# Hybrid decoder step on one core: the output projection's first tile is multiplied, and its second turned, inside the sample stage

## What is computed

```python
h   = rms_norm(x, norm1_g)
proj = h @ w_in                       # attention q, k, v; mLSTM q, k, v, gates
att = dilated attention (8 heads x 64), windows combined by softmax of their log-sums
hb  = mLSTM (4 heads x 128), chunkwise
x   = x + concat(att, hb) @ w_out     # the output projection
x   = x + square(relu(rms_norm(x, norm2_g) @ w_up)) @ w_down
y   = rms_norm(x, norm_f_g)
```

## Time and profile before

| | us |
|---|---|
| median of 3 runs | 2995.48 |
| lowest and highest of them | 2992.3 and 2998.82 |
| the profiled execution | 2989.5 |
| its span, first to last instruction | 2987.7 |

### The profile page before, as it was taken

How to read it: one execution, slowest core, us unless ns; L and a number is a source line. 1 busy time by engine, 2 the same in 40 slices (tenths; PEclk the granted TensorE clock), 3 DMA queues, 4 the chain that set the end, 5 groups by cost and what they waited for, 6 DMA issues and landing times.

```text
span 2987.7 us, 47542 instructions
## 1 busy us (share of the span) xinstructions
PE 2855.3 (96%) x18291; PEld 2478.0 (83%) x18291; DVE 1427.7 (48%) x3363; ACT 926.2 (31%) x1741; POOL 1003.3 (34%) x590
## 2 busy tenths in 40 slices
PE   7999999998999968899999999999999999999997
PEld 5878788887777756678799999989999998899996
DVE  5522555334888845586343333344333333544444
ACT  4301322112767742332132221243212222422222
POOL 1212012211455530210064343444434344545443
PEclk8999999999999988999999999999999999999999
DMA  4322223334464448955352323235222323533332
GB/s 137 113 102 97 97 94 122 106 117 147 133 193 155 160 141 335 370 174 187 134 220 94 126 93 107 94 122 225 94 108 93 126 93 117 207 129 131 138 126 83
DMA packets 124794, 421.41 MB, mean 141 GB/s; under 512 B 18655, under 2 KB 44387, under 8 KB 104918
## 3 DMA queue, kind: packets, MB, share of 16 engines
q1 hardware_dynamic: 103836, 366.53, 34.7%
q10 hardware_dynamic: 19658, 48.68, 4.2%
q0 software_dynamic: 1152, 4.19, 0.5%
HBM read 350.83 MB, written 135.63 MB: 163 GB/s over the span
## 4 chain that ended last, share of the span: by engine, by line
PE 48%; ACT 1%; POOL 1%; DVE 0%; DMA 0%; issue 0%; ACTq 0%
PE mlp_bank L220 16%; PE mlp_bank L221 16%; PE mlp_bank L222 16%; PE mlp_bank L236 0%; PE mlp_bank L235 0%; POOL mlp_wu_lo L2634 0%; DMA mlp_xb<-x 0%; PE mlp_bank L2982 0%; DVE mlp_acc L2854 0%; POOL mlp_xb L2676 0%; ACT mlp_wu_hi L2692 0%; ACT mlp_acc L2767 0%; DVE mlp_hT_lo L2903 0%; DVE mlp_acc L2871 0%; POOL mlp_acc L2681 0%
## 5 line engine op out<-in xcount | busy, mean ns | idle before, releaser
L2854 DVE TENSOR_TENSOR mlp_acc<-mlp_acc,mlp_bank 128x512 f32<-128x512 f32 x542 | 348.2, 684 | 365.7 <-PE mlp_bank L222 357.6
L220 PE MATMUL mlp_bank<-mlp_hT_hi,mlp_wu_hi 128*128 128x384 f32 (+1 forms) x1536 | 496.0, 323 | 3.1 <-PEq L3122 3.1
L222 PE MATMUL mlp_bank<-mlp_hT_hi,mlp_wu_lo 128*128 128x384 f32 (+1 forms) x1536 | 494.6, 322 | 0.0
L221 PE MATMUL mlp_bank<-mlp_hT_lo,mlp_wu_hi 128*128 128x384 f32 (+1 forms) x1536 | 494.4, 322 | 0.0
L2842 DVE TENSOR_TENSOR mlp_xn<-mlp_xn 128x384 f32<-128x384 f32 (+1 forms) x192 | 203.8, 1068 | 509.5 <-ACT mlp_xn L2710 489.3
L220 PE MATMUL mlp_bank<-mlp_wd_hi,mlp_u_hi 128*128 128x512 f32 x1024 | 400.0, 391 | 5.0 <-DVE mlp_acc L2854 5.0
L221 PE MATMUL mlp_bank<-mlp_wd_lo,mlp_u_hi 128*128 128x512 f32 x1024 | 398.9, 390 | 0.0
L222 PE MATMUL mlp_bank<-mlp_wd_hi,mlp_u_lo 128*128 128x512 f32 x1024 | 398.8, 389 | 0.0
L2638 POOL TENSOR_TENSOR mlp_wd_lo<-mlp_wd_raw,mlp_wd_hi 128x2048 fp32r<-128x2048 f32 x48 | 221.8, 4621 | 391.6 <-ACT mlp_wd_hi L2698 391.6
L2647 POOL TENSOR_TENSOR mlp_u_lo<-mlp_xn,mlp_u_hi 128x384 fp32r<-128x384 f32 (+1 forms) x192 | 177.9, 938 | 359.0 <-ACT mlp_u_hi L2719 359.0
L220 PEld LDWEIGHTS mlp_bank<-mlp_hT_hi,mlp_wu_hi 128*128 128x128 f32 x1536 | 288.2, 188 | 5.2 <-issue 3.5
(11 more groups left out here) (370 smaller groups left out, 4693.6 us busy)
## 6 DMA issues: line engine op xcount, KB each, us to landing
mlp_wu_raw<-in_w_up SPq DMA_DIRECT2D x48, 1024.0 KB, 4.9
mlp_wd_raw<-in_w_down SPq DMA_DIRECT2D x48, 1024.0 KB, 4.9
out_win_k_sample<-in_cache_k SPq DMA_DIRECT2D x48, 680.0 KB, 6.3
out_win_v_sample<-in_cache_v SPq DMA_DIRECT2D x48, 680.0 KB, 7.2
p_w_raw<-in_w_tok SPq DMA_DIRECT2D x10, 2048.0 KB
sm_vin<-in_cache_v SPq DMA_DIRECT2D x8, 2048.0 KB, 12.3
proj<-p_stage ACTq DMA_DIRECT2D x53, 256.0 KB, 2.0
parts<-mx_part SPq DMA_DIRECT2D x48, 264.0 KB, 3.9
```

What stands on the lines that cost most here:

```text
L220: nc.tensor.matmul(out, ah, bh, start=(k == 0), stop=False)
L221: nc.tensor.matmul(out, ah, bl, start=False, stop=False)
L222: ins = nc.tensor.matmul(out, al, bh, start=False, stop=(k == n - 1))
L2854: ins = v.tensor_tensor(acc[:, t, 512 * e:512 * e + 512], acc[:, t, 512 * e:512 * e + 512], bank[4 + 2 * (t % 2) + e][:], ALU.add)
```

## The change

- In the sample stage SP issues the weight's last two quarters and the parts of tiles 0 and 1 right behind the values of sequence 6 (in round b = 5), and so ahead of the values of sequence 7. The x rows of tiles 0 to 2 are loaded in the sample stage too, ahead of the 8 stores.
- DVE computes the weights of tile 0 in the second half of sequence 6, its products and sum in the second half of sequence 7. It then also does there the shift of tile 1, lo(0), the rest of the fourth quarter, the combination of tile 1, and lo(1).
- ACT rounds both tiles in the sample stage.
- PE turns tile 0, multiplies its first half, then blocks 0 to 3 of its second half, turns tile 1, and multiplies blocks 4 to 7, all behind the last values product and ahead of the barrier. The output projection's own list starts with products(1, 0).
- The 8 PSUM banks are allocated once for all three stages. The load of tile 2's parts stays in the output projection's block, its condition (tile 0 turned) is met when that block begins.

```diff
@@ class OutHead
+    def load_x(self, sp, t):
+        sp.dma_start(self.xt[t % 3][:], self.K.x[t * P:(t + 1) * P, :]).then_inc(self.x_in[t % 3], 16)
+
+    def turn_first(self, pe, t, bank):
+        pe.wait_ge(self.mixed, t + 1)
+        for k in range(KC):
+            m = (self.ma if k < 4 else self.mb)[t]
+            ins = self.K.nc.tensor.transpose(bank[2 * t + k // 4][:, (k % 4) * P:(k % 4 + 1) * P],
+                                             m[:, (k % 4) * P:(k % 4 + 1) * P], self.K.ident[:])
+        ins.then_inc(self.turned, 1)
+
+    def hi_first(self, act, t, bank):
+        act.wait_ge(self.turned, t + 1)
...
+    def lo_first(self, dve, t, bank):
+        dve.wait_ge(self.hi_ready, t + 1)
...
+    def products_first(self, pe, e, bank, part):
+        cols = slice(512 * e, 512 * e + 512)
+
+        def split(k):
+            if e == 0 and k % 2 == 0:
+                pe.wait_ge(self.w_lo_ready[k // 2], 1)
+
+        if e == 0:
+            pe.wait_ge(self.lo_ready, 1)
+        split_products(self.K.nc, bank[4 + e][:],
+                       [(self.mT_hi[:, 0, k], self.mT_lo[:, 0, k], self.w_hi[:, k, cols], self.w_lo[:, k, cols])
+                        for k in range(KC)], self.prod_mm, split, part=part)
...
@@ mix_sample, block.sync
                 if b:
                     sp.wait_ge(s["summed"], b)
                     load_v(b + 1)
+                if b == 5:
+                    for q in range(2, 4):
+                        O.load_w(sp, q)
+                    for t in range(2):
+                        O.load(sp, t)
...
-            for q in range(2, 4):
-                O.load_w(sp, q)
-            for t in range(2):
-                O.load(sp, t)
+            sp.wait_ge(s["summed"], DEC_B - 1)
+            for t in range(3):
+                O.load_x(sp, t)
             sp.wait_ge(s["o_ready"], DEC_B)
@@ block.scalar
+            O.exp(act, 0)
             probs(DEC_B - 1)
-            O.exp(act, 0)
             O.round(act, 3)
+            O.hi_first(act, 0, bank)
+            O.exp(act, 1)
+            O.hi_first(act, 1, bank)
@@ block.vector
             for b in range(4, DEC_B):
                 first_half(b)
-                second_half(b - 1)
...
+                second_half(b - 1, first_weights if b == DEC_B - 1 else None)
+            second_half(DEC_B - 1, lambda: O.blend(dve, O.chain, 0))
+            O.shift(dve, O.chain, 1)
+            O.lo_first(dve, 0, bank)
+            O.rest(dve, v, 3)
+            O.combine(dve, O.chain, 1)
+            O.lo_first(dve, 1, bank)
@@ block.tensor
             second_half(DEC_B - 1)
+            O.turn_first(pe, 0, bank)
+            O.products_first(pe, 0, bank, range(KC))
+            pe.wait_ge(s["o_ready"], DEC_B)
+            O.products_first(pe, 1, bank, range(4))
+            O.turn_first(pe, 1, bank)
+            O.products_first(pe, 1, bank, range(4, KC))
@@ project_out
-            for t in range(3):
-                load_x(t)
...
-            hi(0)
-            O.exp(act, 1)
...
-            O.rest(dve, v, 3)
-            lo(0)
-            O.shift(dve, chain, 1)
-            O.combine(dve, chain, 1)
...
-            turn(0)
-            for t in range(NP + 1):
+            for t in range(1, NP + 1):
                 products(t, 0)
```

More of the change, by code:

```diff
@@ L1614, in __init__ @@
         self.shifted, self.exps, self.mixed, self.own = (sem("out_" + n) for n in ("shifted", "exps", "mixed", "own"))
+        self.x_in = [sem(f"out_x_in{q}") for q in range(3)]
+        self.turned, self.hi_ready, self.lo_ready, self.prod_mm = (
+            sem("out_" + n) for n in ("turned", "hi", "lo", "prod_mm"))
     def load_w(self, sp, q):
@@ L1655, in combine, with blend @@
         chain.link(v.tensor_tensor(S[:, 2], S[:, 1], S[:, 4, 2:3].broadcast_to([P, 3, H]), ALU.mult))
+    def combine(self, dve, chain, t):
+        self.weights(dve, chain, t)
+        self.blend(dve, chain, t)
+    def blend(self, dve, chain, t):
+        v, p = self.K.nc.vector, t % 2
+        q, S = self.pt[p], self.st[:, p]
+        prod = self.prod if t else self.prod_first
         for a in range(3):
@@ L1830, in mix_sample @@
         sm = rec("sm", NS, 10, MH)
-        bank = [ctx.enter_context(nc.psum_tensor(f"sm_bank{i}", [P, 512], F32)) for i in range(8)]
+        bank = K.bank
         SC, PV, ML = (3, 4), 5, (6, 7)
@@ L2542, in mlp @@
         assert nc.sbuf_base <= K.front_at + 4 * TOP
-        bank = [ctx.enter_context(nc.psum_tensor(f"mlp_bank{i}", [P, 512], F32)) for i in range(8)]
+        bank = K.bank
         acc_in, y_out, copied = sem("mlp_acc_in"), sem("mlp_y_out"), sem("mlp_copied")
@@ L3045, in mixers @@
         K.end_stage(kept)
+        K.bank = [K.ctx.enter_context(K.nc.psum_tensor(f"bank{i}", [P, 512], F32)) for i in range(8)]
         mix_sample(K)
```

43 lines of the change are left out of this document (22 added, 21 removed).

## The result

| | before, us | change, us |
|---|---|---|
| median (20 runs each, same chip) | 2995.55 | 2999.96 |
| lowest and highest | 2992.30 and 3002.59 | 2993.44 and 3008.68 |
| the profiled execution | 2989.5 | 3002.55 |
| its span | 2987.7 | 3000.8 |

The ratio is 1.0017, 95% interval 1.0010 to 1.0023: the change costs 4.4 us at the median, between 3.0 and 6.9. The forecast was 4.0 us and 2999.5. That is a difference smaller than the 0.2% named ahead of time, but with 20 runs on each side it is one.

A forecast was written before the change was run, and what follows sets the result against it. PE is busy 96% of the span, so its idle or slow places count. A 5.5 us lead is spent on tile 2's 5.9 us wait, then DVE's list makes it 4.0 us later: 2993.5 profiled, median 2999.5, range 2993.5 to 3004.5.

The forecast's parts named there:

- Step 1: End of sample stage: values of sequence 7 queue behind 4.24 MB, land at 1264.2; last values product starts 4.0 us late.
- the rival of the jammed queue: SP's held issues let the DMA engines run dry, values land at 1268; +7.8 us, 3003.3; chance 0.13.
- Step 2: Last values product on PE, partly at low clock after idling: 4.9 us (bounds 3.2 to 5.5), ending at 1269.1.
- Step 3: Tile 0 without the barrier: turn, rounding and rest take 3.5 us; its first product starts at 1272.6.
- Step 4: PE's work up to the barrier 12.3 us, barrier 1.2 us; output projection's block starts at 1286.1, 5.5 us ahead.
- Step 5: Tile 2's parts, loaded behind the barrier, are ready 11.6 us after the block's start; PE stands still for 5.9 us.
- Step 6: DVE's list behind tile 2's combination takes 10.9 us and decides; tile 2's first product comes 4.0 us later.
- The rule against the rows: Skill's HBM limit of about 358 GB/s against the measured 391: 4.24 MB would take 11.8 us, sum 1.5 us more.
- undelayed values: Rival: transfers ahead of the last values land by 1254, clock stays up; 1.7 us earlier, 2993.8; chance 0.13.
- slower transfers: Rival: rows of about 2 KB move at 360 GB/s instead of 410, values land at 1265.7; 3001.0; chance 0.06.
- The low clock through turn and first half: Rival: PE's clock stays low through tile 0's turn and first half; about +11 us, 3006; chance 0.05.
- Tile 2 did hold PE: Against the rival that tile 2 doesn't hold PE: 5.5 us faster, 2990.0, or 2984.3 with undelayed values; chance 0.08.

The follow-up runs named there:

- the second profile: The change, unaltered, profiled once more; from the values product of sequence 6 to `mlp` 237.90 us, against 239.31 in its first profile.
- e6: Kernel before, with only the loads of the weight's last two quarters and rows of tiles 0 and 1 moved ahead of sequence 7's values; ratio to before 0.9995.
- e8: The change, with its loads of the rows and of the weight back behind the last values; ratio to before 1.0031.

## Why the prediction was right

- **Step 1, the late values.** Said: 4.0 us late, idle from 1259.7 to 1264.2. Measured: 3.97 us late (9.50 against 5.53), 4.50 us idle, ended by the DMA. The transfers did stand in line. The landing named for 1264 comes at about 1267, because the whole stretch began 3.0 us later in this execution; by the distance it is as said. SP's issues were held much longer than before (7.96 us), as the rival of the jammed queue had it, but that rival's condition, values of 7 issued after about 1254, wasn't met: with 3 us for the later start they would have had to come after 1257, and they came at 1248.28. The transfers in the queue outlasted the hold, as the 416 and 406 GB/s of the windows up to the landing show.
- **Step 2, the values product.** Said 4.9 us; measured 4.38 (1267.21 to 1271.17 and 0.42), and in the second profile 4.58. The low clock comes with part of it (0.58 and 0.57 in two windows).
- **Step 3, no barrier ahead of tile 0.** The turn follows at once, the gap is 2.50 us as before. First product said 17.9, measured 17.40 and 17.50.
- **Step 4, up to the barrier.** Said 12.3 + 1.2 us; measured 14.9 in the first profile, 13.3 in the second. The second is the term as it was worked out. The first has the clock at 0.50 in part of the first half, which the sum had at full speed. Block start said 31.4, measured 32.29 and 30.83.
- **Step 5, tile 2.** Said: rows 6.2 us behind the block's start, idle 5.9 us. Measured: 7.63 us (1290.00 to 1297.63), idle 7.23; the second profile has 7.68 and 7.28. **This term was sized too small, by 1.4 us.** I took the page's median landing of 5.1 from the steady part of the stage; here the transfer stands behind `mlp_gain` and lands after 6.8, which is outside the 4.7 to 6 that I had allowed.
- **Step 6, DVE's list decides.** Said 10.9 us; measured 1303.01 to 1313.87, 10.86. The measuring point was to move by 4.0 us: it moved by 4.9 and 6.4. From there on the delay neither grew nor shrank (+6.38 at `mlp`, +4.97 in the second profile), as said. The forecast of 4.0 us is nearer to the 4.4 of the timed runs than to either profile, whose distances lie inside the runs' interval as well (3.0 to 6.9): that it is off by only 0.4 is in part luck.
- **The rule against the rows.** By 358 GB/s the values would have come 1.5 us later than my sum; they came within 0.1 us of it, and the windows read 416 and 406 GB/s. The measurement decides: the row was the right basis. The 425 GB/s that the Trainium skill (DMA: Bandwidth & Descriptors, Bandwidth) gives for one core by itself is nearer to them.

The rivals: undelayed values and slower transfers didn't occur. The low clock through turn and first half did so in part, for 1.5 us and in one execution of two. Tile 2 did hold PE. One slip in the chances changes nothing here: by the rivals' own figures, 0.70 lie within 0.2% and 0.08 are faster, where the text has 0.71 and 0.07.

What the prediction didn't weigh apart is the two halves of the change. e6 and e8 part the change: its loads alone -0.7 us of the stretch, its compute alone +8.1. They don't quite add up to the +5.0 to +6.4 of the change. In the change the block starts earlier than in e8 (32.29 and 30.83 against 34.23), and tile 2's load with it. The turn of tile 0 comes only 0.1 to 0.2 us earlier; the rest is the clock, at 0.50 in e8 from 1272 to 1280, behind PE's wait of 5.32 us.

## What to carry to other kernels

Work pulled across a barrier brings what is left behind nearer to its user: the first load behind a barrier, with the list of the engine that consumes it, must come along, or the gain ends in a wait two tiles on (here 16.3 us from the landing, whatever happens ahead). What was hidden behind other work then stands in one line with it, and each delay ahead of the barrier is passed on in full, as the late values were in the change and weren't in e6. So test a suspected delay in the new order, and don't take from one repair that helps that the others are small. Look for what becomes late next not once but until nothing is: tile 2's load, tile 2's combination, tile 3's load behind the gain's; only with all of them moved did the 9.5 us by which tile 0 is turned earlier arrive at the end. And when loads are put in another order, ask also when their consumers on POOL and DVE will run, and beside what.
